# The key turn and the output transposes of a gated delta rule, moved one weight chunk earlier

## The reference, cut to what matters

```python
q, k, v = l2norm(heads(q)), l2norm(heads(k)), heads(v)
beta = jax.nn.sigmoid(b_raw)
g_log = -jnp.exp(a_log) * jax.nn.softplus(a_raw + dt_bias)
o_a = gated_delta_chunked(q, k, v, g_log, beta)
o_a = rmsnorm(o_a, g_dn_out).reshape(B, S, DN_WIDTH) * jax.nn.silu(z_a)
y_a = o_a @ w_br_a

# inside gated_delta_chunked, for each head and each chunk of tokens
A = (k * beta) @ k.T * decay * strict
T = inverse of (eye + A)                 # unit lower triangular
u, w = T @ (v * beta), T @ (k * beta * exp(gc))
v_new = u - w @ S
o = q_dec @ S + (q @ k.T * decay) @ v_new
S = S * exp(g_last) + k_end.T @ v_new
```

## Time and profile before

| | us |
|---|---|
| median of three runs | 2748.1 |
| lowest and highest | 2747.83 and 2754.2 |
| the profiled execution | 2747.83 |
| its span, first to last instruction | 2746.2 |
| TensorE busy in the span | 2684.7 |
| VectorE busy | 1703.9 |
| ScalarE busy | 1236.6 |
| GpSimd busy | 157.6 |
| mean granted TensorE clock | 0.992 |

### The profile page before, as it was taken

One profiled execution on the slowest core, in us unless ns is written; L12 is line 12 of the kernel. 1 busy time (PEld: TensorE's weight loads), 2 busy tenths in 40 slices (PEclk: granted clock), 3 DMA queues, 4 the chain that ended last, 5 costly groups with the idle time before them and its releaser, 6 DMA issues.

```text
span 2746.2 us, 40779 instructions
## 1 busy us (share of the span) xinstructions
PE 2684.7 (98%) x14610; PEld 2335.1 (85%) x14610; DVE 1703.9 (62%) x2260; ACT 1236.6 (45%) x1473; POOL 157.6 (6%) x331
## 2 busy tenths in 40 slices
PE   8999999999999999999989999999999999999997
PEld 7888888888888888888889989899998989878886
DVE  5555555555455555554566566574888888866564
ACT  5444444444444444444455445353434434364453
POOL 0000000000000000000004031331000000000000
PEclk9999999999999999999999999999999999999999
DMA  7555555555555555556545454444555555555654
GB/s 246 184 177 180 178 177 180 178 182 186 191 192 190 191 193 187 191 200 196 194 129 180 138 169 155 152 157 150 189 186 179 180 185 185 172 180 192 225 173 142
DMA packets 150004, 495.04 MB, mean 180 GB/s; under 512 B 28496, under 2 KB 29232, under 8 KB 149360
## 3 DMA queue, kind: packets, MB, share of 16 engines
q1 hardware_dynamic: 147376, 482.25, 53.9%
q0 software_dynamic: 2496, 10.87, 1.3%
HBM read 489.89 MB, written 3.16 MB: 180 GB/s over the span
## 4 chain that ended last, share of the span: by engine, by line
PE 94%; DVE 2%; DMA 1%; ACT 1%; issue 1%; SPq 0%; POOL 0%; DVEq 0%; POOLq 0%; ACTq 0%
PE PS L1511 23%; PE PS L1512 23%; PE PS L1513 23%; PE PS L1525 6%; PE PS L1528 6%; PE PS L1527 6%; PE PS L1687 2%; PE PS L1536 1%; DMA raw<-in_stream 1%; ACT whi L531 1%; PE PS L1694 1%; DVE wlo L893 0%; PE PS L1706 0%; PE PS L1581 0%; PE PS L1714 0%
## 5 line engine op out<-in xcount | busy, mean ns | idle before, releaser
L893 DVE TENSOR_TENSOR wlo<-raw,whi 128x1024 fp32r<-128x1024 f32 x900 | 1100.7, 1226 | 981.6 <-ACT whi L531 975.6
L531 ACT CAST whi<-raw 128x1024 fp32r<-128x1024 f32 x900 | 943.3, 1051 | 1385.0 <-PE PS L1513 1022.7
L1511 PE MATMUL PS<-whi,aH 128*128 128x512 f32 x1792 | 702.3, 392 | 3.6 <-DVE wlo L893 2.0
L1512 PE MATMUL PS<-wlo,aH 128*128 128x512 f32 x1792 | 697.9, 389 | 0.0
L1513 PE MATMUL PS<-whi,aL 128*128 128x512 f32 x1792 | 697.8, 389 | 0.0
L1528 PE MATMUL PS<-aH,wlo 128*128 128x256 f32 x1536 | 438.9, 286 | 8.6 <-issue 8.6
L1525 PE MATMUL PS<-aH,whi 128*128 128x256 f32 x1536 | 443.8, 289 | 2.8 <-DVEq L1309 1.7
L1527 PE MATMUL PS<-aL,whi 128*128 128x256 f32 x1536 | 438.1, 285 | 0.0
L1511 PEld LDWEIGHTS PS<-whi,aH 128*128 128x128 f32 x1792 | 336.8, 188 | 74.3 <-DVE wlo L893 2.9
L1513 PEld LDWEIGHTS PS<-whi,aL 128*128 128x128 f32 x1792 | 336.6, 188 | 70.5
L1512 PEld LDWEIGHTS PS<-wlo,aH 128*128 128x128 f32 x1792 | 336.9, 188 | 68.1
(11 more groups left out here) (290 smaller groups left out, 2198.3 us busy)
## 6 DMA issues: line engine op xcount, KB each, us to landing
raw<-in_stream SPq DMA_DIRECT2D x900, 512.0 KB, 3.3
H<-in_x SPq DMA_DIRECT2D x4, 512.0 KB, 8.1
pB<-in_pool_b POOLq DMA_DIRECT2D x4, 512.0 KB, 4.1
iT<-diag_in SPq DMA_DIRECT2D x16, 128.0 KB, 3.9
bg<-in_b_gate POOLq DMA_DIRECT2D x8, 256.0 KB, 4.0
out<-eb SPq DMA_DIRECT2D x4, 512.0 KB, 2.9
dmask<-in_dmask POOLq DMA_DIRECT2D x1, 1536.0 KB, 10.4
dT<-cum_rows SPq DMA_DIRECT2D x6, 256.0 KB, 4.4
```

The source lines that it names most:

```text
L531: nc.scalar.copy(whi[:, s], raw[:, s]).then_inc(hi_done, 1)
L893: nc.vector.tensor_tensor(wlo[:, s], raw[:, s], whi[:, s].bitcast(F32), ALU.subtract).then_inc(lo_done, 1)
L1511: mm(out, hi[:, kt + k, tok], whi[:, s, k], start=kt + k == 0, stop=False)
L1512: mm(out, hi[:, kt + k, tok], wlo[:, s, k], start=False, stop=False)
```

## The change

In passes 1 to 3 the key turn and all that follows from it up to `ke` stands one step earlier: step 11, 12 and 13 in place of 12, 13 and 14. In pass 0 only `ke` moves, from 14 to 13. The tail of the previous pass moves with it: the products on `oD` from `LV + 12` to `LV + 11`, its transposes and the split into `oaH` and `oaL` from `LV + 14` to `LV + 13`. The buffer `half_up`, a constant 0.5 for GpSimd's square roots, gets a place of its own for the whole program and is filled at its start; one wait and one semaphore count go.

```diff
+        half_up = sb(outer, "half_up", [P, 8])
-                half_up = sb(r, "half_up", [P, 8])
@@ GpSimd
+            nc.gpsimd.memset(half_up[:], 0.5)
-            pool.wait_ge(t_lo, (T_P + 8) * QT)
-            nc.gpsimd.memset(half_up[:], 0.5).then_inc(const_set, 1)
-            pool.wait_ge(const_set, 3)
@@ ScalarE
-                if n == LV + 14:
+                if n == LV + 13:
                     t_split_hi(i + T_D, oaH, i * QT, lambda c: C_DN)
-                    if j == 12:
+                    if j == (12 if first else 11):
                         act.wait_ge(k_ps, i + 1)
                         nc.scalar.activation(gm[:]..., PS[:, 6:8], ACT.Square).then_inc(sq_sb, 1)
@@ VectorE
-                if n == LV + 12:
+                if n == LV + 11:
                     dve.wait_ge(ors_sb, i + 1)
                     dve.wait_ge(zd_sb, i + 1)
                     ...  # oD <- oD * norm * gate
-                if n == LV + 14:
+                if n == LV + 13:
                     t_split_lo(i + T_D, oaH, oaL, i * QT, lambda c: C_DN)
-                    if j == 12:
+                    if j == (12 if first else 11):
                         norms(i, 0)
                         key_scales(i)
-                    if j == 13:
+                    if j == (13 if first else 12):
                         ...  # ed, aT
-                    if j == 14:
+                    if j == 13:
                         ...  # ke
-                dve.wait_ge(const_set, 4)
+                dve.wait_ge(const_set, 3)
@@ TensorE
-                if n == LV + 14:
+                if n == LV + 13:
                     pe.wait_ge(od_sb, i + 1)
                     transpose_tiles(oD)
-                    if not first and j + D_PER < LV + 14:
+                    if not first and j + D_PER < LV + 13:
                         delta_late(i - 1, j + D_PER)
-                    if j == 12:
+                    if j == (12 if first else 11):
                         pe.wait_ge(kqv_sb, i * 3 + 1)
                         ...  # the key turn
-                    if not first and j + D_PER == LV + 14:
+                    if not first and j + D_PER == LV + 13:
                         pe.wait_ge(ke_sb, i * 2 + 2)
                         delta_late(i - 1, j + D_PER)
```

## The result

The changed kernel is slower: a median of 2774.8 us over four runs (2771.8 to 2781.0) against 2750.3 us before, a ratio of 1.0091 (95% interval 1.0068 to 1.0113). That is 24.5 us, where 5.3 had been forecast, and outside the range. The profiled execution took 2764.5 us, with a span of 2762.8 us, and is faster than all four timed runs.

The account below looks back on a forecast made before the run. TensorE, busy 98% of the span, was taken to bound the kernel. To the profiled 2747.8 us only the new kqv wait was added, 3 x 1.76 = 5.3, giving 2753.1 us; range 2746 to 2760.

Parts of the forecast that it names:

- The wait for ke: Delta stage, passes 1 to 3: oD's transposes still wait 3.05 us for ke, three times; nothing gained or lost.
- the forecast's chain: VectorE ahead of oD's transposes: low part, oD products, aT products, another low part, ke; 7.64 us long, unchanged.
- The key turn: Passes 1 to 3: the moved turn waits for kqv from ScalarE's Silu, 1.76 us each, 5.3 us lost in all.
- The diagonal blocks: SyncE's queue: aT's blocks are reloaded 2.7 us later, GpSimd's inverse loses 1.0 us against TensorE; cost nothing.
- the cover of 2.2 us: Slack left, of 3.2 us, between the end of GpSimd's inverse and the queue taking up its result.
- The place of half_up: Its new place shifts later buffers' addresses by 32 bytes; 1 us either way allowed.
- The clock: Rival, delta stage: the three waits for ke bring one clock fall each, 10.4 us slower, 2758.2 us; chance 0.17.

Follow-up runs that it names:

- the order alone: The changed kernel with half_up left in its old place, steps still moved, timed against the kernel before: 2753.1 us, ratio 1.0026, 6.6 us slower.
- the place alone: The kernel before with only half_up in its new place, buffers behind it 32 bytes further on, no step moved: 2765.3 us, ratio 1.0069, 18 us slower.
- the runs with 128 and 256 bytes: The kernel before with only a spare buffer of that size a partition behind mhalf: 2760.2 us, ratio 1.0053 with 128; 2747.0 us, ratio 1.0001 with 256.

## Why the prediction was wrong

**The wait for ke: right.** It was to stay at 3.05 us, three times; it is 9.2 us in three. In pass 1, for the earlier trace rows, TensorE's turn and its transposes, and VectorE's first and last member of the chain:

```profile
1574.05 1.06 PE L1692 MATMUL PS<-con,kqv 128*128 128x128 f32 x8 [1.78 <-ACT kqv L766]
...
1588.58 1.93 PE L1534 MATMUL PS<-con,oD 128*128 128x128 f32 x8 [3.06 <-DVE ke L1279]
```

```profile
1580.89 1.23 DVE L891 TENSOR_TENSOR wlo<-raw,whi 128x1024 fp32r<-128x1024 f32 x1 [2.65 <-ACT whi L529]
...
1587.41 1.11 DVE L1279 TENSOR_SCALAR ke<-PS,ed 128x128 f32<-128x128 f32 x4
```

ke ends at 1587.41 + 1.11 = 1588.52, 7.63 us after the low part's start; the forecast's chain was 7.64. That the chain itself is the wait was then shown by taking two members out of it.

**The key turn: right.** 1.76 us per pass were forecast; the transposes of kqv had 1.78 us of idle before them. ScalarE ahead of it, for the earlier trace rows:

```profile
1571.46 1.28 ACT L766 ACT_TABLE_LOAD   x1
1572.76 1.06 ACT L766 ACTIVATE kqv<-yD 128x1024 f32<-128x1024 f32 x1
```

Table load and Silu stand where they stood, and the turn waits for their end at 1573.82. It is partly luck that 1.76 came out so closely. Chunk 11 ended at 1574.05 - 1.78 = 1572.27, so the Silu's end was 1.55 us behind it, where 1.71 had been reckoned; and the turn started 0.23 us behind the Silu's end, where 0.05 had been reckoned. The two errors cancel, and what fills the 0.23 us isn't shown. The step's sum of 5.3 us is that in the list of waits, and the order alone measured 6.6.

**The diagonal blocks: right.** Store and reload on the queue, for the earlier trace rows:

```profile
1597.06 1.85 SPq L367 DMA_DIRECT2D diag_in<-aT  x4
...
1601.04 1.71 SPq L372 DMA_DIRECT2D iT<-diag_in  x4
```

The reload starts 1601.04 - 1588.58 = 12.5 us after the start of the transposes of oD; 10.8 had been reckoned. The stretch behind these transposes ran at a clock of 0.58 here (below), which lost 4 x 0.42 = 1.7 us, the whole difference. Where only the order was changed no fall stands there: the transposes start at 1578.58, and the reload comes 1589.36 - 1578.58 = 10.8 us later.

```profile
1589.36 1.71 SPq L372 DMA_DIRECT2D iT<-diag_in  x4
```

(The terms that the prediction names for the store add up to 1585.0, not 1585.2; it changes nothing.) The waits for iT and at the loop's turn did not grow, 3.4 and 2.8 us against 4.1 and 2.9, so the cover of 2.2 us held.

**The place of half_up: the step that failed.** The prediction gave the 32 bytes 1 us either way, from no row. They cost 18 us. The trace of before could have given the scale: of TensorE's 14610 matmuls some 3100 wide ones read a stationary operand that the shift moves, so each nanosecond on one is worth 3 us. What no row of it could say is that there would be a nanosecond: it took a second layout to see that.

The Trainium skill has a rule by which one would call it free. TensorE: Matmul & The Clock Gate, in Step-by-step: what each phase is for, says that TensorE reads the stationary and the moving operand through two ports of their own, and that loading the next weights takes no bandwidth from the running product. By that rule, read as one on placement too, the time would have been that of the order alone, 2753. The runs disagree as far as the pace goes: with all buffers shifted alike nothing changed; with only the distance between the two operands changed, each wide product took 6 ns more. Whether it is the read of the next weights that holds up the running product was not tried.

**The clock.** It was the rival for slower, and it isn't the cause, but it explains the spread. In the profiled execution of the changed kernel one of the three waits for ke was followed by a fall of the granted clock to its lower level. The row gives the stretch in us, then the busy time of PE, PEld, DVE, ACT and POOL, then the granted clock (0.58), the DMA share and GB/s:

```profile
1588.00:1592.00 4.00, 3.42 (x16) 3.42 (x17) 2.87 (x7) 1.68 (x4) 0.00 (x0) 0.58 0.69 228
```

Its mean clock is 0.996, that of its timed runs 0.990 to 0.993, and before had 0.992 in its profiled execution. 2762.8 x 0.004 is 11 us of lost full speed, 2746.2 x 0.008 is 22. With the 11 us between the two added, the 16.6 between the profiled spans become 27.6, where the medians have 24.5. Over the 57 runs of the kernel before beside the experiments the time was 2744.5 us on average at a mean clock of 0.993 (16 runs) and 2750.0 at 0.991 (11 runs): 5.5 us for 0.002, what the clock alone gives (2746 x 0.002).

The prediction held against this rival that in one trace the clock stayed full through the three waits of 3.05 us. One trace is too little for that. Eleven of the kernels timed here, before and after among them, have these three waits. In their profiled executions a fall began during such a wait or within 1.5 us of its end in 21 of 33 cases: in none of three before, in one after, in all three with the place alone. So whether a fall stands near these waits differs from trace to trace, and the one trace that was read had none.

## What to carry to other kernels

A buffer that is moved or added is an edit to every product behind it: after such a change compare the mean length of each group of matmuls by operands, in the stages that were not touched, before looking for waits. Where a kernel is at its best pace, keep the distance of the two operands of TensorE what it was when a small buffer comes in ahead of large ones (here by filling up to 256 bytes), or put it behind them. When a step and all it waits for and is waited for by are moved together, its wait moves with it; what shortens it is to take out of the chain what the waiting engine doesn't need.

## What the runs showed of the hardware

- With the moving operand 512 columns wide, in this reduced format, the groups have means of 389 to 392 ns (one product starts every 227 ns) when the stationary operand is a multiple of 256 bytes from the moving one, and 394 to 398 ns (one every 233 ns) at 32, 64 or 128 bytes past that. For aH and the weights the multiple of 256 is certain, since only buffers of 16 KB lie between them; for the o buffers it is worked out, with each small buffer rounded up to 32 bytes, and the runs with 128 and 256 bytes agree. The products of vH with sTH and sTL, 394 and 395 ns with the place alone at an unchanged distance, show that this isn't the whole of it.
- With 256 columns and the roles of the two buffers changed, 32 bytes make it faster: 117 ns from start to start in place of 120.
- Absolute addresses did not matter: all buffers 32 bytes on, ratio 1.0005 (0.9995 to 1.0015). What in the chip makes the distance count was not tried.
- A fall of the clock began during a TensorE wait of 3.05 us or within 1.5 us of its end in 21 of 33 cases over eleven traces, and the mean clock differs from run to run of the kernel before between 0.990 (2753.3 us on average) and 0.995 (2740.3).
